# The odd layer's gated output projection by seven quarter products, with the gate applied by VectorE afterwards

## What is computed

```python
x = x + gate * (mix @ od_w_out_2)              # the projection of this case
rows = rms_norm(x) * (1 + scale) + shift       # what the router and the experts read
...                                            # router: best group, best two experts of a token
x = x + gate2 * sum_of_two_experts(rows)
```

## Time and profile before

| | us |
|---|---|
| median of three runs | 2024.54 (2023.17 to 3323.06) |
| the profiled execution | 2022.98 |
| its span, first to last instruction | 2021.2 |
| the stage's first product after the meeting | 1756.70 |
| first product of the experts' first tile | 1840.30 |

### The profile page before, as it was taken

How to read it: one execution, slowest core, us unless ns; L and a number is a source line. 1 busy time by engine, 2 the same in 40 slices (tenths; PEclk the granted TensorE clock), 3 DMA queues, 4 the chain that set the end, 5 groups by cost and what they waited for, 6 DMA issues and landing times.

```text
span 2021.2 us, 28938 instructions
## 1 busy us (share of the span) xinstructions
PE 1893.0 (94%) x10950; PEld 1038.0 (51%) x10950; DVE 1188.9 (59%) x1908; ACT 642.9 (32%) x1274; POOL 249.4 (12%) x260
## 2 busy tenths in 40 slices
PE   7999999999999999899998999899997999999993
PEld 4554875544444444455645764533334678645330
DVE  2001777487787653358754643677756657456774
ACT  2011762200000001242313641266643556323551
POOL 3000110011111000012200002511102000041101
PEclk9999999999999999999999999999998989999997
DMA  8632100677766442411111002689965020148995
GB/s 267 161 84 83 54 12 22 224 253 252 240 237 235 150 171 94 133 42 42 42 42 47 18 19 89 260 323 365 361 246 209 1 84 2 35 163 347 385 416 199
DMA packets 108472, 323.88 MB, mean 160 GB/s; under 512 B 9063, under 2 KB 43015, under 8 KB 89904
## 3 DMA queue, kind: packets, MB, share of 16 engines
q1 hardware_dynamic: 77920, 190.56, 26.3%
q0 software_dynamic: 25168, 112.53, 15.6%
q10 hardware_dynamic: 5248, 18.94, 2.4%
HBM read 291.48 MB, written 35.76 MB: 162 GB/s over the span
## 4 chain that ended last, share of the span: by engine, by line
PE 72%; DVE 7%; issue 7%; DMA 6%; PEld 4%; PEldq 2%; ACT 1%; POOL 1%; POOLq 0%; DVEq 0%; SPq 0%; ACTq 0%
PE ps L3435 15%; PE ps L466 7%; PE ps L2056 6%; PE ps L2866 6%; PE ps L1186 5%; PE ps L1232 4%; PE ps L3236 4%; PE ps L1207 4%; PE ps L364 3%; DMA X<-moe_rows,row_token 3%; PE ps L2887 3%; PE ps L335 2%; PE ps L2032 2%; PEld ps L1779 2%; PE ps L1779 1%
## 5 line engine op out<-in xcount | busy, mean ns | idle before, releaser
L3435 PE MATMUL ps<-wide 128*128 128x512 f32 (+1 forms) x736 | 306.5, 575 | 1.9 <-issue 1.7
L3435 PEld LDWEIGHTS ps<-wide 128*128 128x128 f32 x736 | 138.3, 190 | 166.3 <-issue 164.1
L2866 PE MATMUL ps<-wide,X 128*32 x448 | 197.5, 594 | 2.1 <-DVE X L3037 2.1
L2866 PE MATMUL ps<-Z,X 128*32 128x512 f32 x1344 | 197.9, 594 | 0.0
L2056 PE MATMUL ps<-wide 128*128 128x512 f32 (+1 forms) x384 | 149.1, 545 | 0.5 <-issue 0.5
L1540 DVE SCALAR_TENSOR_TENSOR Z<-Z,wide 128x2048 f32<-128x2048 f32 x56 | 131.6, 2350 | 2.8
L1186 PE MATMUL ps<-T 64*128 64x256 f32 (+1 forms) x888 | 110.0, 378 | 8.7 <-DVE nm L1325 6.8
L1779 PE MATMUL ps<-wide 128*128 128x512 f32 x256 | 113.8, 602 | 2.1 <-issue 1.1
L744 ACT ACTIVATE T<-ps 128x512 f32<-128x512 f32 (+2 forms) x139 | 70.7, 536 | 131.0 <-PE ps L1779 111.5
L1257 ACT ACTIVATE T<-T,nm 128x768 f32<-128x768 f32 (+3 forms) x112 | 86.7, 775 | 77.6 <-DVE nm L1325 77.6
L2866 PEld LDWEIGHTS ps<-wide,X 128*32 128x32 f32 x448 | 47.0, 110 | 124.1 <-issue 124.1
(11 more groups left out here) (421 smaller groups left out, 3353.8 us busy)
## 6 DMA issues: line engine op xcount, KB each, us to landing
wide<-in_experts SPq DMA_DIRECT2D x64, 1024.0 KB, 10.7
Z<-in_mod_w POOLq DMA_DIRECT2D x32, 1024.0 KB, 5.3
T<-in_experts SPq DMA_DIRECT2D x32, 1024.0 KB, 11.1
X<-in_mod_w POOLq DMA_DIRECT2D x16, 1024.0 KB, 5.4
moe_out<-X ACTq DMA_DIRECT2D x28, 512.0 KB
wide<-in_w_down SPq DMA_DIRECT2D x12, 1024.0 KB, 6.8
wide<-in_w_gate SPq DMA_DIRECT2D x22, 512.0 KB, 5.9
wide<-in_w_up SPq DMA_DIRECT2D x22, 512.0 KB, 6.9
```

What stands on the lines that cost most here:

```text
L2866: last = pe.matmul(ps[rows, t % 2, :], mo.xT[:, c, rows], w_rows, start=(c == 0), stop=(c == DK - 1))
L3435: last = pe.matmul(self.gu.bank(u)[:, columns], w, self.rhs(c)[:, columns], start=(c == 0), stop=(c == DK - 1))
```

## The change

The odd layer's projection becomes a class of its own, `GatedBySeven`. The input's rows (K halves: chunks 0 to 3 and 4 to 7; tile parity: tiles 0, 2 and tiles 1, 3) and the weights (K halves by column halves: `b11`, `b12`, `b21`, `b22`) are cut in quarters, and the product is made of seven quarter products, P1 to P7, instead of eight. Each is four products for each of two tiles: 56 in all, 8 of them (P1) in `begin`. The quarters' sums (S1 to S4 of 128 x 1024, T1 to T4 of 128 x 2048) are made by VectorE. ScalarE copies P1 into four halves of two tiles' results in SBUF; VectorE adds P2, P3, P6 and P5 to them (L874 of the changed kernel), multiplies each of the four results by the gate and adds it to X, and then does the same with P7 and P4 as they come, for tiles 1 and 3. The raising of the row gains, for this layer, moves from the stage's start to behind T3. The norm's first pair is turned behind the last product. The weight ring passes over two places, in which T1 and T2 are kept.

```diff
--- before.py
+++ after.py
@@ -736,6 +736,212 @@
+class GatedBySeven(Stage):
...
+    SUMS = "S1", "S2", "S4", "T1", "T2", "S3", "T3", "T4"
...
+        self.PARTS = [(p, i) for p in ("P1", "P2", "P3", "P6", "P5") for i in range(n)] + [(p, i) for i in range(n) for p in ("P7", "P4")]
...
+    def tile_done(self, eng, t):
+        if t % 2:
+            self.after_add(eng, "P4", t // 2, "total")
+        else:
+            self.after_add(eng, "total", t // 2, 0)
...
+    def begin(self, pe, tiles):
+
+        self.k.rg.await_landed(pe, self.b11)
+        for i in range(self.n):
+            self.part(pe, "P1", i, self.rows(0, 0), self.b11)
+
+    def tensor(self, pe):
...
+        for i in range(n):
+            self.part(pe, "P2", i, self.rows(1, 0), self.b21)
+        rg.await_landed(pe, self.b22)
+        self.after_sum(pe, "S4")
+        for i in range(n):
+            self.part(pe, "P3", i, self.s4, self.b22)
+        self.after_sum(pe, "T2")
+        for i in range(n):
+            self.part(pe, "P6", i, self.s2, self.t2, 0 if i else 1)
+        for i in range(n):
+            self.part(pe, "P5", i, self.s1, self.t1)
+        self.after_sum(pe, "T4")
+        for i in range(n):
+            self.part(pe, "P7", i, self.s3, self.b12, 0 if i else 1)
+            self.part(pe, "P4", i, self.rows(1, 1), self.b21, 0 if i else 2)
+            if i:
+                self.norm.turn(pe, i - 1)
+        pe.drain().then_inc(k.weights_used, 2)
+        self.between(pe, self.norm)
+        self.norm.tensor(pe)
+
+    def vector(self, dve, ch):
...
+        made(self.s1, self.rows(0, 1), self.rows(1, 1), ALU.add)
+        self.after_sum(dve, "S1")
+        made(self.s2, self.s1, self.rows(0, 0))
+        self.after_sum(dve, "S2")
+        made(self.s4, self.rows(1, 0), self.s2)
...
+        made(t1, b12, b11)
+        self.after_sum(dve, "T1")
+        made(t2, b22, t1)
+        for i in range(n):
+            self.after_part(dve, "P2", i)
+            self.after_copy(dve, i)
+            add(("P2", i), self.result(2 * i)[:, 0:512], self.bank("P2", i))
+        made(self.s3, self.rows(0, 0), self.rows(0, 1))
+        made(b12, b22, b12)
+        self.row_stores.raise_gains(dve)
+        for i in range(n):
+            self.after_part(dve, "P3", i)
+            add(("P3", i), self.result(2 * i)[:, 512:D], self.bank("P3", i))
+        self.after_sum(dve, "T2")
+        made(b21, b21, t2)
+        for i in range(n):
+            self.after_part(dve, "P6", i)
+            add(("P6", i, 0), self.result(2 * i)[:, 512:D], self.bank("P6", i))
+            add(("P6", i, 1), halves(self.result(2 * i + 1)), twice("P6", i))
+        for i in range(n):
+            self.after_part(dve, "P5", i)
+            add(("P5", i, 0), self.result(2 * i)[:, 512:D], self.bank("P5", i))
+            add(("P5", i, 1), self.result(2 * i + 1)[:, 512:D], self.bank("P5", i))
...
+            for row in (0, 1):
+                t = 2 * i + row
+                add(("gated", i, row), self.result(t), gate, ALU.mult)
+                add(("total", i, row), k.X[:, t, :], self.result(t))
+        for i in range(n):
+            gate, x = self.gates[:, 0 if 2 * i < ST else 1, :], k.X[:, 2 * i + 1, :]
+            self.after_part(dve, "P7", i)
+            multiply(("P7", i, "gated"), halves(self.product), twice("P7", i), halves(gate))
+            add(("P7", i, "total"), x, self.product)
+            if i:
+                self.norm.tile(dve, ch, 2 * i - 1)
+            self.after_part(dve, "P4", i)
+            multiply(("P4", i, "gated"), self.product[:, 0:512], self.bank("P4", i), gate[:, 0:512])
+            add(("P4", i, "total"), x[:, 0:512], self.product[:, 0:512])
+            self.norm.tile(dve, ch, 2 * i)
+            if i:
+                self.norm.take(dve, "dve", i - 1)
+        self.norm.tile(dve, ch, 2 * n - 1)
+        self.norm.vector(dve, ch)
+
+    def scalar(self, act, ch):
+        for i in range(self.n):
+            self.after_part(act, "P1", i)
+            both = self.k.Z[:, 5120 + 2 * D * i:5120 + 2 * D * (i + 1)].rearrange("p (a n) -> p a n", a=4)
+            act.activation(both, self.bank("P1", i).unsqueeze(1).to_broadcast((P, 4, 512)), ACT.Copy).then_inc(self.k.firsts_copied.sem, 1)
         self.norm.scalar(act, ch)
@@ -2436,6 +2642,10 @@
     def vector(self, dve, ch):
+        if self.l == 0:
+            self.raise_gains(dve)
+
+    def raise_gains(self, dve):
         k = self.k
...
@@ -3907,7 +4119,7 @@
-        odd.then = Linear(k, hT, DK, A["od_w_out_2"][0], D, seq, gated_take(oddgate), ["dve"] * 8, norm=mod_sets(1, 1, False))
+        odd.then = GatedBySeven(k, A["od_w_out_2"][0], seq, mod_sets(1, 1, False), oddgate)
         moe(1, seq, [row_stores(1, odd.then, 1), odd.then], lambda y, w: Combine(k, seq, y, out[0], w))
```

More of the change, by code:

```diff
@@ L3664, in two_blocks @@
         k.sums_made, k.partials_added, k.parts_full = tally("sums_made"), tally("partials_added"), tally("product_parts_full")
+        k.firsts_copied = tally("first_products_copied")
         k.mods_ready = sem("mods_ready")
@@ L3881, in two_blocks @@
         add(Together(k, Load(k, [(k.X[:, :, :], away)]), even))
+        gate_rows = Loading(k, gate_loads(0, 2, 2))
         even.then = Linear(k, hT, DK, A["ev_w_out_2"][0], D, allt, gated_take(k.gatebc), ["dve"] * 12,
                            norm=mod_sets(0, 1, True))
-        head = [Loading(k, gate_loads(0, 2, 2)), row_stores(0, even.then, 2), even.then]
+        head = [gate_rows, row_stores(0, even.then, 2), even.then]
         oddgate = k.Z[:, 9920:9920 + D].unsqueeze(1)
```

84 lines of the change are left out of this document (added).

## The result

| | before | after |
|---|---|---|
| median, us | 2025.05 | 2033.01 |
| ratio, 95% interval | | 1.0036 [1.0027, 1.0046] |
| profiled execution, its span | 2022.98, 2021.2 | 2031.15, 2029.4 |
| the stage: first record of `begin` to the counting | 1745.90 to 1821.29: 75.39 | 1747.65 to 1832.28: 84.63 |
| `begin` to the experts' first product | 1745.90 to 1840.30: 94.40 | 1747.65 to 1849.68: 102.03 |

The change costs some 7 us, 0.4%; the prediction was 2032.0. One of the 18 executions before and two of the 18 after took 3323 to 7580 us: the ratio leaves them out (medians without them 2024.90 and 2032.10), and since the first profile of the changed kernel was of one of them, the profile shown is of a second run. The router's lines in the changed kernel are 210 higher than before, the others 206.

The account below looks back on a forecast made before the run. The prediction took TensorE's products, then the router's steps, as the bound before, and VectorE's tail and router meeting GpSimd after. 2022.98 + 8.4 (counting later) + 0.6 (idle products, clock) = 2032.0 us; range 2021 to 2037.

Parts of the forecast that it names:

- TensorE's end, the sums, VectorE's lateness: Projection: products end at 1794.8, the sums hide completely, and VectorE's first scaling at 1798.1 makes it later by 3 us.
- GpSimd and VectorE collide: Behind the products: VectorE steps with two SBUF operands, or scaling one, stand until GpSimd's running step ends; counting +8.4 us.
- the three waits of the rows: Profile before: VectorE's add to X, scaling and 16-column step end 0.56, 0.55 and about 0.05 us behind GpSimd steps.
- pass between two GpSimd tiles: VectorE's tail: P4's gating and total for tile 3 run unheld between two GpSimd tiles, ending at 1807.0.
- The turn at half speed hides under GpSimd: Norm's turn on TensorE, after about 10 us idle: runs at the lower clock but costs no time.
- That the router's steps stand behind GpSimd until 1825.4: Router: its small steps, 5.25 us, wait for GpSimd's fourth add, so counting starts near 1829.7, +8.4 us.
- The 56 idle products: TensorE behind the counting: 6.4 us at full clock, 12.9 at half, 7.93 before; taken as +0.6 us.
- The gather: Behind the counting: row stores land by 1835.6, the gather comes at 1840.9, so waiting for them costs nothing.
- small steps pass (1): Router: only long VectorE steps stand behind GpSimd, the router runs from the second turn; +4.7, 2027.7 us; chance 0.13.
- there is no collision (2): VectorE's tail: its steps keep finding gaps between GpSimd's, second turn 1.7 us earlier than before; 2021.3 us; chance 0.14.
- TensorE stays the bound (3): Projection: gatings hide beside P7 and P4, so the whole 6.9 us saved shows; 2016.1 us; chance 0.05.
- the clock stays low behind the counting (4): TensorE: the 56 idle products run wholly at 1.2 GHz, 12.9 us, +5.0; 2036.4 us; chance 0.10.

Follow-up runs that it names:

- after_busy: Changed kernel with 40 idle products between TensorE's last P4 and the first pair's turn: median 2033.85 us, ratio 1.0038 to the kernel before.
- split_rows: Changed kernel with each of GpSimd's row steps of 1024 columns cut into two of 512: ratio 1.0031 to the kernel before.
- after_norows: Changed kernel without GpSimd's multiply and add for the odd layer's rows: 2025.86 us, ratio 0.9999 to the kernel before.
- norows_busy: Changed kernel without the odd layer's GpSimd row steps, with 24 idle products ahead of the first turn: median 2024.32 us, ratio 0.9993.
- folded_split: Seven products with the gate multiplied into the weights by GpSimd, and GpSimd's row steps cut into halves of 512 columns: ratio 0.9972.

## Why the prediction was right, and where its path wasn't

Counted from `begin`, which the prediction has at 1745.90.

*TensorE's end, the sums, VectorE's lateness: right.* The meeting came after 7.40 us (7.4 foretold), the last product ended after 48.84 (48.9), no sum was waited for, the first tile was scaled after 51.6 (52.2) and GpSimd's first multiply began after 52.7 (53.2).

*GpSimd and VectorE collide: right, and shown.* Taking GpSimd's steps away takes 8.5 us off the stage. That the three waits of the rows agree with the rule "to 0.05 us" holds for the 16-column step alone, which ends 0.04 us behind GpSimd's; the other two end 0.56 and 0.55 behind, less than their own 0.69 and 0.75 us. The accounting was off in one place: the total of tile 3's P4 was to "pass between two GpSimd tiles"; it took 3.17 us, held though its record begins 0.24 us before that of GpSimd's multiply. With it, tile 2's and tile 3's scalings slid: the last ended after 69.3 us for 66.6.

*"The turn at half speed hides under GpSimd": right* for the turn (`after_busy`), but the prediction missed what else is slow. The logits (1.93 us) and the 18 idle records (4.09 us) also stand ahead of the second turn on TensorE's queue. The rows for it were ready after 69.3 us; it began after 73.1.

*That the router's steps stand behind GpSimd until 1825.4: not in this execution.* With the second turn 6.4 us later than foretold, the router started when GpSimd was done; only the 16-column step was held, to 1.38 us. Two delays lie side by side and end within a microsecond or two: with the second turn 0.9 us earlier the 16-column step stood 2.28 us (`after_busy`), and with it 5.6 us earlier the router's steps stood behind GpSimd (`split_rows`). Of these steps 8 of 22 are reductions of one operand, so "nearly all on two SBUF operands" says too much. GpSimd's fourth add ended after 77.7 us for the 79.5 foretold. The sum let GpSimd lose 1.8 us on top of tiles of 6.57 us; a tile that nothing holds takes 6.24 (1800.38 to 1806.62 in the kernel before), so 1.0 of it was in the price of three tiles already, and from its first issue to its last add GpSimd took 25.6 us for the 26.9 of the sum. The counting came after 84.6 us, for 83.8: **+9.2 us, where the forecast said +8.4.** That the two are so near is partly luck: the forecast went by the router behind GpSimd, and the execution by the second turn behind slow records on TensorE's queue.

*The 56 idle products: the mis-sized term.* They ran at full speed, 6.31 us on the chain for 7.93 before, -1.6 and not +0.6: the granted clock was 1.00 from 1821.60 on, ahead of them. The account had TensorE idle again ahead of the counting; it idled 1.9 us there, as before, since 32 idle products that the account left out stand ahead of it too. (Nor does +0.6 come out of the row that it names: there the clock was low for 5.4 us behind the idle time, 844.00 to 849.40, which would be +1.2.) The two errors partly cancel: +7.6 us to the experts' first product, +8.2 in the span, 7 in the measured ratios, for +9.0 in the sum. That 2032.0 itself meets the median is luck again: the sum starts from an execution 2 us faster than the median before, which makes up for the 2 us that it has too many.

*The gather* waited for the list, not for the stores, as foretold: GpSimd's wait for them ended at 1835.07, the gather is at 1841.87.

*The rivals.* That small steps pass (1) falls with `split_rows`, that there is no collision (2) with `after_norows`, that TensorE stays the bound (3) with the chain, that the clock stays low behind the counting (4) with the 6.31 us.

The whole, from single stages: with no row steps on GpSimd, 73.22 before, 65.29 folded, 76.13 changed. Seven products for eight give 7.9 us; gating on VectorE, with the order that goes with it, costs 10.8, of which `norows_busy` puts some 1.2 on the clock; and what GpSimd's steps cost more than before adds 6.3. -7.9 + 10.8 + 6.3 = +9.2. Counted to the experts' first product the same three are -7.7 + 12.3 + 3.1 = +7.6, and by the ratios -8.3 + 10.3 + 5.1 = +7.1. So VectorE's added work and its order are the larger part of the loss by every count, and the collision is 3 to 6 us of it.

## What to carry to other kernels

Saved products are worth something only if what follows them isn't made later by the same change: ask when each engine *behind* the stage can begin, not only when TensorE ends. VectorE steps that read two SBUF operands or scale one, and GpSimd's steps, should be counted as one queue; here it paid to give the gating to GpSimd, but a hundred microseconds earlier, on the weights. Products that fill TensorE's time stand in its queue like any others, and at the lower clock they took up to 1.8 times as long here (4.09 us for 2.27).

## What the runs showed of the hardware

- By the records, a VectorE step that begins up to 0.57 us ahead of a GpSimd step can be held by it: 0.24 at 1807.20 in the changed kernel, 0.57 at 1821.73 in `split_rows`. In those moments GpSimd was issuing a DMA. The issue alone doesn't hold: in `norows_busy` a total of 1024 columns, begun during one at 1798.40, took 1.23 us. Which of the two engines' steps is admitted then stays open.
- The Trainium skill's page "SBUF — State Buffer", section "SBUF: two separate sides", gives the hold as one of a whole instruction. Most holds here end 0.03 to 0.6 us behind one GpSimd instruction, or 1.1 for a step of 1024 columns on two operands. But two multiply halves issued without a wait between them held as one instruction would, twice in `split_rows` (3.53 and 3.17 us) and three times in `folded_split` (3.56, 2.70 and 2.95 us); add halves never did. What decides it wasn't tried further.
- GpSimd pays too: its add took 3.21 us for 2.35 where a 1024-column total got in first, and 2.68 where a scaling did.
